# A product-key search whose last step is split between VectorE and GpSimd

## What is computed

```python
q = (xb @ w_query).reshape(t, 8, 2, 128)
s = einsum('thik,hink->thin', q, sub_keys)            # 2 x 128 scores per token and head
v_half, i_half = top_k(s, 16)                         # 16 best of each half
cand = v_half[:, :, 0, :, None] + v_half[:, :, 1, None, :]          # 16 x 16 sums
cand_idx = i_half[:, :, 0, :, None] * 128 + i_half[:, :, 1, None, :]
top_v, top_pos = top_k(cand, 16)                      # 16 best pairs
idx = take_along_axis(cand_idx, top_pos)              # <- the part that changes
g = softmax(top_v)
act = gelu(einsum('thkd,td->thk', expert_u[idx], xb))
out = einsum('thk,thkd->td', g * act, expert_v[idx])
```

## Time and profile before

| what | us |
|---|---|
| median of 3 runs | 2610.92 |
| lowest, highest | 2607.22, 2611.05 |
| the profiled execution | 2620.58 |
| its span in the trace | 2618.8 |
| TensorE busy (share of the span) | 2305.7 (88%) |
| VectorE busy | 1801.4 (69%) |
| GpSimd busy | 1169.0 (45%) |
| ScalarE busy | 638.1 (24%) |
| data moved | 705.28 MB, mean 269 GB/s |
| chain that ended last: PE, DVE, POOL, DMA, issue, ACT | 37%, 19%, 14%, 11%, 11%, 7% |

### The profile page before, as it was taken

The page is one execution under the profiler, slowest core; times in us unless marked ns, Lnnn a source line. Parts: engine busy times, 40 slices in busy tenths (PEclk is TensorE's granted clock), DMA queues, the critical chain, the costliest instruction groups (busy, mean ns, idle before and its releaser), DMA issues.

```text
span 2618.8 us, 26507 instructions
## 1 busy us (share of the span) xinstructions
PE 2305.7 (88%) x8779; PEld 1454.0 (56%) x8779; DVE 1801.4 (69%) x3184; ACT 638.1 (24%) x1564; POOL 1169.0 (45%) x978
## 2 busy tenths in 40 slices
PE   6988888998899998899989988977999999999930
PEld 1545454454467443477568877856666666644410
DVE  2657676645501888777778997578766676757698
ACT  2334435331211113311321112199111100100010
POOL 0022222221000347666532334556548878676675
PEclk8999999999999998899999999999999999999975
DMA  8211101117575669999775679989999999999998
GB/s 303 73 33 57 40 24 40 49 60 272 195 269 182 229 254 383 361 339 415 287 265 185 225 257 334 348 305 362 352 394 411 412 386 418 347 419 378 419 395 296
DMA packets 235577, 705.28 MB, mean 269 GB/s; under 512 B 22910, under 2 KB 47614, under 8 KB 234052
## 3 DMA queue, kind: packets, MB, share of 16 engines
q0 software_dynamic: 117792, 428.92, 42.6%
q1 hardware_dynamic: 116948, 272.27, 27.9%
q10 hardware_dynamic: 720, 2.62, 0.2%
HBM read 690.23 MB, written 13.50 MB: 269 GB/s over the span
## 4 chain that ended last, share of the span: by engine, by line
PE 37%; DVE 19%; POOL 14%; DMA 11%; issue 11%; ACT 7%; SPq 1%; DVEq 0%; ACTq 0%; POOLq 0%; another core or an unknown queue 0%
PE bank L959 14%; POOL arena L1786 6%; POOL arena L1778 5%; DMA arena<-in_peer_v,arena 5%; PE bank L1181 4%; PE bank L808 4%; DMA arena<-in_peer_u,arena 3%; PE bank L853 2%; ACT arena L1674 2%; DVE arena L1964 2%; PE bank L1111 2%; DVE arena L2181 2%; POOL arena L1832 2%; DVE arena L2203 2%; DVE arena L2127 1%
## 5 line engine op out<-in xcount | busy, mean ns | idle before, releaser
L1778 POOL DMA_INDIRECT arena<-in_peer_u,arena x384 | 486.3, 1266 | 624.7 <-DVE arena L2181 346.0
L2203 DVE SCALAR_TENSOR_TENSOR arena<-arena 128x1024 f32<-128x1024 f32 x381 | 498.4, 1308 | 123.2 <-DMA arena<-in_peer_v,arena 113.6
L2181 DVE CUSTOM_DVE_ANT_0 arena<-arena 128x1024 f32<-128x1024 f32 x384 | 475.9, 1247 | 149.5 <-DMA arena<-in_peer_u,arena 147.5
L1786 POOL DMA_INDIRECT arena<-in_peer_v,arena x384 | 462.0, 1203 | 242.0 <-DVE arena L2203 132.4
L959 PE MATMUL bank<-arena 128*128 128x512 f32 (+1 forms) x1472 | 510.5, 509 | 21.8 <-issue 8.1
L1181 PE MATMUL bank<-arena 128*128 128x256 f32 x2048 | 457.2, 381 | 18.5 <-ACT arena L1633 17.8
L1219 PE MATMUL bank<-arena 128*128 128x512 f32 x1024 | 455.8, 598 | 7.2 <-DMA arena<-in_peer_v 4.0
L1181 PEld LDWEIGHTS bank<-arena 128*128 128x128 f32 x2048 | 391.7, 191 | 101.0 <-issue 49.4
L959 PEld LDWEIGHTS bank<-arena 128*128 128x128 f32 x1472 | 284.1, 194 | 244.1 <-issue 206.3
L1219 PEld LDWEIGHTS bank<-arena 128*128 128x128 f32 x1024 | 196.4, 192 | 228.1 <-issue 217.1
L1633 ACT ACTIVATE arena<-bank 128x256 f32<-128x256 f32 x128 | 49.0, 384 | 597.1 <-PE bank L1181 535.1
(11 more groups left out here) (259 smaller groups left out, 2469.6 us busy)
## 6 DMA issues: line engine op xcount, KB each, us to landing
arena<-in_peer_ut SPq DMA_DIRECT2D x128, 512.0 KB
arena<-in_peer_v SPq DMA_DIRECT2D x128, 512.0 KB
arena<-in_w_in SPq DMA_DIRECT2D x22, 2048.0 KB
arena<-in_w_ada_t POOLq DMA_DIRECT2D x32, 512.0 KB, 3.8
arena<-in_w_ssd_out SPq DMA_DIRECT2D x8, 2048.0 KB
arena<-in_w_query SPq DMA_DIRECT2D x8, 2048.0 KB
arena<-in_w_ada SPq DMA_DIRECT2D x4, 2048.0 KB, 16.3
arena<-in_w_fourier SPq DMA_DIRECT2D x4, 2048.0 KB
```

The lines of the kernel that those rows point to most:

```text
L1778: nc.gpsimd.indirect_dma_start(rowbuf[slot], None, a["peer_u"], bass.IndirectOffsetOnAxis(ap=entries(IDX, k), axis=0)).then_inc(row_in[slo ...
L1786: nc.gpsimd.indirect_dma_start(rowbuf[slot], None, a["peer_v"], bass.IndirectOffsetOnAxis(ap=entries(IDX, k), axis=0)).then_inc(row_in[slo ...
L2181: V.tensor_tensor_reduce(out=rowbuf[slot], in0=rowbuf[slot], in1=h2c if item < PH else h2a[:, item // PH - 1, :], scale=1.0, scalar=0.0, o ...
L2203: STT(pv, rowbuf[slot], w, pv, ALU.mult, ALU.add).then_inc(s("vc_used"), 1)
```

## The change

The end of the search is computed in another form and in two places. The table of places now holds 16-bit values and is spread out to 1024 elements (four groups of 16 places x 16 picks), with the pick innermost. VectorE copies the split positions to 16 bits, compares them with the table, and adds one to a new semaphore `marked`. GpSimd, in `picks_for`, waits for `marked`, multiplies the result with the indices, sums over the places by halving (8, 4, 2, then the last two), combines the halves for row tiles, and counts `topk_done` or `topw_done`. For row tiles the factor 128 is put into the indices beforehand, by a small product in place of the copy of L2152. Each GpSimd step waits for the one before it (`pch`). VectorE, before it writes the indices of a search, waits for GpSimd to be done with the search before. A function `searches_before` says how many of these passes GpSimd makes before each row: all of whose searches lie on VectorE ahead of the step that frees the row's slot. The expanded table takes the place of constants of the scan (they now share one tensor, `scan_consts`) and is written by two instructions at the start of the lookup, after the scores of tile 0 are there.

```diff
+def searches_before(kind, k):
+    ...
+    passed = sum(c < context or a < apart for _, c, a in SEARCHES)
+    return max(passed, SEARCH_OF[k // TOPK] + 1)
...
-        convw = sb("convw_sb", [P, 24, TAPS])
+        scan_consts = sb("scan_consts", [P, 512])
+        convw = scan_consts[:, 192:192 + 24 * TAPS].rearrange("p (i k) -> p i k", k=TAPS)
-        places = sb("places", [P, 4, TOPK], U32)
+        places = scan_consts.bitcast(BF16).rearrange("p (g m k) -> p g m k", g=4, k=TOPK)
...
+            def picks_for(kind, k):
+                while picks_done[0] < searches_before(kind, k):
+                    m, (items, _, _) = next(picked)
+                    n, (t, h) = len(items), divmod(items[0], PH)
+                    e4 = cands[:, 0:256 * n].bitcast(BF16).rearrange("p (g m k) -> p g m k", g=2 * n, k=TOPK)
+                    number = i16fs[:, 0:2 * n * TOPK].rearrange("p (g m) -> p g m", g=2 * n)
+                    pool.wait_ge(s("marked"), m + 1)
+                    pch(TT(e4, e4, number.unsqueeze(3).broadcast_to([P, 2 * n, TOPK, TOPK]), ALU.mult))
+                    for m_left in (8, 4, 2):
+                        pch(TT(e4[:, :, 0:m_left], e4[:, :, 0:m_left], e4[:, :, m_left:2 * m_left], ALU.add))
+                    if t in WHOLE:
+                        TT(ij_all[...], e4[:, :, 0, :], e4[:, :, 1, :], ALU.add).then_inc(s("topw_done"), n)
+                    else:
+                        pch(TT(picks[...], e4[:, :, 0, :], e4[:, :, 1, :], ALU.add))
+                        pch(TT(picks[:, 0:n * TOPK], picks[:, 0:n * TOPK], picks[:, n * TOPK:2 * n * TOPK], ALU.add))
+                        nc.gpsimd.tensor_copy(entries(IDX, ...), picks[:, 0:n * TOPK]).then_inc(s("topk_done"), n)
+                    picks_done[0] = m + 1
...
             def u_row(k):
+                picks_for("u", k)
                 row_free("u", k)
...
-                CP(i16fs[:, 0:2 * n * TOPK], i16s[:, 0:2 * n * TOPK])
+                if searched["last"]:
+                    dve.wait_ge(s(searched["last"]), searched[searched["last"]])
+                if t in WHOLE:
+                    CP(i16fs[:, 0:2 * n * TOPK], i16s[:, 0:2 * n * TOPK])
+                else:
+                    TT(i16fs[...], i16s[...], radix.unsqueeze(2).broadcast_to([P, 2, n * TOPK]), ALU.mult)
...
-                ch(TT(e4, place..., flat(tijs)..., ALU.is_equal))
-                ch(TT(e4, e4, flat(i16fs)..., ALU.mult))
-                if t in WHOLE:
-                    V.tensor_reduce(ij_all[...], e4, AX.X, ALU.add).then_inc(s("topw_done"), n)
-                else:
-                    ch(V.tensor_reduce(flat(picks), e4, AX.X, ALU.add))
-                    STT(entries(IDX, ...), half[0], float(NKEY), half[1], ALU.mult, ALU.add).then_inc(s("topk_done"), n)
+                ch(CP(tij16s[:, 0:2 * n * TOPK], tijs[:, 0:2 * n * TOPK]))
+                TT(e4, places[:, 0:4:3 - n], flat(tij16s)..., ALU.is_equal).then_inc(s("marked"), 1)
...
             dve.wait_ge(s("sc_free"), 4)
+            CP(places[:, 2:4], row16)
+            ch(TS(places[:, 0:2], row16, float(TOPK), None, ALU.mult))
             top(0)
```

More of the change, by code:

```diff
@@ L223, with searches @@
 APART_TOP_AT = {42 if n == 4 else START_BETWEEN if n == 6 else 16 * n - 14: (n, n + 1) for n in range(4, 2 * PH, 2)}
+def searches():
+    at = [((0,), 0, 0), ((1,), 0, 0)] + [(pair, j + 1, 0) for j, pair in TOPS_AT.items()]
+    c, a = STEPS_DONE + 8, 0
+    for h in range(PH):
+        at.append(((3 * PH + h, 4 * PH + h), c, a))
+        c = min(CSTEPS, c + CTX_BESIDE[h])
+        if h in APART_TOP_BESIDE:
+            at.append((tuple(PH + n for n in APART_TOP_BESIDE[h]), c, a))
+        a += APART_BESIDE[h]
+    return at + [(tuple(PH + n for n in pair), CSTEPS, j + 1) for j, pair in sorted(APART_TOP_AT.items())]
+SEARCHES = searches()
+SEARCH_OF = {item: n for n, found in enumerate(SEARCHES) for item in found[0]}
+def searches_before(kind, k):
+    context, apart = 0, 0
+    before = ROW_BEFORE[ROW_NUMBER[kind, k]]
+    if before is not None:
+        kind_before, k_before = ROW_ORDER[before]
+        if k_before < PICKS:
+            context = k_before + 1 + (kind_before == "v") * LEAD
+        else:
+            apart = k_before - PICKS + 1 + (kind_before == "v") * APART_LEAD
+    passed = sum(c < context or a < apart for _, c, a in SEARCHES)
+    return max(passed, SEARCH_OF[k // TOPK] + 1)
 GATES_FIRST = (28, 36, 51)
@@ L2138, in scores_of @@
                 return src.rearrange("p (h n) -> p h n", h=2)
+            searched = {"topk_done": 0, "topw_done": 0, "last": None}
             def top(*items):
@@ L2151, in top @@
                         best16(v16[:, half, q, :], i16[:, half, q, :], src[:, half, :], sw2[:, half, :])
-                CP(i16fs[:, 0:2 * n * TOPK], i16s[:, 0:2 * n * TOPK])
+                t, h = divmod(items[0], PH)
+                if searched["last"]:
+                    dve.wait_ge(s(searched["last"]), searched[searched["last"]])
+                searched["last"] = "topw_done" if t in WHOLE else "topk_done"
+                searched[searched["last"]] += n
+                if t in WHOLE:
+                    CP(i16fs[:, 0:2 * n * TOPK], i16s[:, 0:2 * n * TOPK])
+                else:
+                    TT(i16fs[:, 0:2 * n * TOPK].rearrange("p (h k) -> p h k", h=2),
+                       i16s[:, 0:2 * n * TOPK].rearrange("p (h k) -> p h k", h=2),
+                       radix.unsqueeze(2).broadcast_to([P, 2, n * TOPK]), ALU.mult)
                 ch(TT(cand, v16[:, 0].unsqueeze(3).broadcast_to([P, n, TOPK, TOPK]),
@@ L2156, in top @@
                     best16(tv[:, q, :], tp[:, q, :], cands[:, 256 * q:256 * q + 256], cand2)
-                t, h = divmod(items[0], PH)
                 over = (d_w[:, :, TOPK * h:TOPK * h + TOPK] if t in WHOLE else
@@ L2162, in top @@
                       ALU.bitwise_and))
-                e4 = cands[:, 0:256 * n].bitcast(BF16).rearrange("p (g k m) -> p g k m", g=2 * n, m=TOPK)
-                place = places[:, 0:4:3 - n, :]
-                ch(TT(e4, place.unsqueeze(2).broadcast_to([P, 2 * n, TOPK, TOPK]),
-                      flat(tijs).unsqueeze(3).broadcast_to([P, 2 * n, TOPK, TOPK]), ALU.is_equal))
-                ch(TT(e4, e4, flat(i16fs).unsqueeze(2).broadcast_to([P, 2 * n, TOPK, TOPK]), ALU.mult))
-                if t in WHOLE:
-                    V.tensor_reduce(ij_all[:, :, TOPK * h:TOPK * h + TOPK], e4, AX.X, ALU.add).then_inc(s("topw_done"), n)
-                else:
-                    ch(V.tensor_reduce(flat(picks), e4, AX.X, ALU.add))
-                    half = picks[:, 0:n * TOPK], picks[:, n * TOPK:2 * n * TOPK]
-                    STT(entries(IDX, items[0] * TOPK, n * TOPK), half[0], float(NKEY), half[1],
-                        ALU.mult, ALU.add).then_inc(s("topk_done"), n)
+                ch(CP(tij16s[:, 0:2 * n * TOPK], tijs[:, 0:2 * n * TOPK]))
+                e4 = cands[:, 0:256 * n].bitcast(BF16).rearrange("p (g m k) -> p g m k", g=2 * n, k=TOPK)
+                TT(e4, places[:, 0:4:3 - n], flat(tij16s).unsqueeze(2).broadcast_to([P, 2 * n, TOPK, TOPK]),
+                   ALU.is_equal).then_inc(s("marked"), 1)
             def u_dot(k):
```

28 lines of the change are left out of this document (21 added, 7 removed).

## The result

The change takes **2705.65 us** (median of 4 runs, 2704.18 to 2725.17) where the kernel before takes 2610.99: a ratio of **1.0382, 95% interval 1.034 to 1.0424**. Such a ratio is made from all the runs and is not quite the quotient of the medians (here 1.0363), so a difference of two versions in microseconds comes out up to some 7 us apart by the two ways. The forecast was 2658, range 2600 to 2682: the direction was right, the size half of what came. The profiled execution took 2725.17, 19.5 above its median (that of before 9.7), so differences between the two traces overstate by some 10 us.

A forecast was written before the change was run, and what follows sets the result against it. Up to 1600 VectorE's lateness was taken to reach TensorE; the last part was bound by row and block transfers. Terms 17 + 10.7 + 20 = +47 on 2611 gave 2658 us, range 2600 to 2682.

The forecast's parts named there:

- The moved constants cost nothing: Constants moved to make room for the expanded table: no cost; only the two instructions writing the table cost, 1.3 with waits.
- VectorE's saving of 48 us: Over 21 searches VectorE is relieved of 48 us: 2.25 or 2.45 per pair, 1.4 per single item.
- GpSimd's pass undisturbed: Product and sums on GpSimd without collisions: 5.0 us for a pair of tiles 3 and 4, 6.2 for row tiles.
- Turns: Behind every search GpSimd and VectorE exclude each other; each pass step waits out one row step of about 1.2 us.
- Behind h = 0: Pairs h = 0 to 3: the fifth step's row comes 13.1 us behind the search, +4.3 each, +17.
- 850 to 997: First stage: late rows behind the pairs release ACT, and so TensorE at 997, 10.7 us later.
- the squares: Pairs up to 1600: +17 us at the squares, and TensorE's blocks end that much later.
- The pair searched at 1623 is covered by the 21.5 us of slack: VectorE's wait at 1706 for the blocks to end, 21.52 us, covers this pair's pass.
- The last part: Five pairs behind 1850: GpSimd resumes rows 9.3 us later, losing 4.0 us of transfers each, +20 us.
- the passes hide: Rival, chance 0.18: passes with turns take under about 3.8 us, rows resume no later than before, 2577 us.
- do not collide: Rival, chance 0.10: passes cost 6.2 and 5.0 us but no turns occur, 2609 us.
- GpSimd is the bound in the last part: Rival, chance 0.10: GpSimd's queue never catches up, five passes count in full, 46 in place of 20, 2684 us.

The follow-up runs named there:

- all on VectorE: The change with product and tree run on VectorE behind the comparison, not on GpSimd: 1.013; with the arena on byte 24320, 1.0042.
- all passes late: The change with GpSimd's passes mostly behind 4 to 10 further rows: 1.0137 (arena on 24096), 1.0149 (24128), 1.007 (24320).
- the arena back: The change with 224 unused bytes ahead of the arena, putting it on byte 24320 as in the kernel before: 2681.40 us, 1.0234.

## Why the prediction was half right

**"The moved constants cost nothing" is the step that failed.** The merged tiles moved the arena off its multiple of 256, and where the DMA engines are all busy they move 403 GB/s in place of 418. The window of before behind 1850:

```profile
1850.00:2619.00 769.00, 656.27 (x2024) 385.04 (x2022) 550.79 (x806) 67.24 (x139) 536.73 (x440) 0.93 0.97 387
```

Estimated from it: 387 GB/s over 769 us are 298 MB; at 403 in place of 418 that takes 26 us more. By the ratios it is 37 us for the kernel before moved by 32 bytes and 25 moved by 128, 23 for all on VectorE (1.013 against 1.0042), 39 for the change (1.0382 against 1.0234), but only 17 to 21 with all passes late (1.0137 and 1.0149 against 1.007). No term, rival or bound held this. With the arena back the change is at 1.0234, 61 us above before, and 2611 x 1.0234 = 2672 lies inside the range.

**The rest, +47 forecast, +61 measured**, by the terms:

- *VectorE's saving of 48 us*: right in size and eaten. The `u_dot`s grew from 475.9 to 496.9 us in all, the `v_add`s from 498.4 to 521.2. VectorE's busy time is 1806.9 beside 1801.4.
- *GpSimd's pass undisturbed*: 1.85 was taken for the product; 1.92 measured, and 1.7 by what it holds VectorE up; 2.4 for three halvings with their gaps, 2.41 measured. By the Trainium skill (GPSIMD Engine Reference, Elementwise — side-by-side cycle accounting: 4497 ns for 2048 elements in 32 bits) the product would be 2.25, an estimate; the 1.85 from GpSimd's own rows was nearer.
- *Turns*: right, instruction by instruction (the fence behind the pair (2,3)). It is what the Trainium skill (SBUF — State Buffer, Who interferes with whom) calls a lock held for the whole instruction; the trace agrees: 1.7 us of waiting beside the product.
- *Behind h = 0*, where the forecast put the fifth step 13.1 us behind the search:

```profile
1390.56 2.88 POOL L1820 TENSOR_TENSOR arena<-arena 128x1024 bf16<-128x1024 bf16 x1 [22.89 <-DVE arena L2237]
1393.53 4.13 POOL L1822 TENSOR_TENSOR arena<-arena 128x512 bf16<-128x512 bf16 x3
1397.80 1.10 POOL L1824 TENSOR_TENSOR arena<-arena 128x64 f32<-128x64 bf16 x1
1399.05 0.98 POOL L1848 DMA_INDIRECT arena<-in_peer_v,arena  x1
...
1390.40 6.22 DVE L2267 SCALAR_TENSOR_TENSOR arena<-arena 128x1024 f32<-128x1024 f32 x3
...
1403.44 1.28 DVE L2267 SCALAR_TENSOR_TENSOR arena<-arena 128x1024 f32<-128x1024 f32 x1 [4.71 <-DMA arena<-in_peer_v,arena]
```

  13.04, with a wait of 4.71 where 4 to 6 stood. The searches h = 1 and 2 come 4.0 and 4.3 us later each (4.3 was forecast), the pair behind h = 2 only 2.2. From h = 0 to h = 7 the change loses 11.8 us, 13.1 with the arena back; forecast 17.
- *850 to 997*: forecast 10.7. TensorE is released at 1017.41, 19.7 later, and at 1006.74, 9.1 later, with the arena back; taken from the first search of each trace 18.1 and 10.9. The first row behind the pair (2,3) is used 14.1 us behind it (14.8 was forecast), but a second wait for a row, 5.29 us at 916.86, was not foreseen: with four slots the round of rows starts late and goes on late. How much of the spread between traces is this and how much chance stays open.
- *997 to h = 0*: no search lies there, and the forecast has nothing. In the five traces with the arena on a multiple of 256 and passes on GpSimd, 6.6 to 14.6 us are lost there (11.5 by the change with the arena back), in the twelve others -4.9 to 3.0. No run explains it. So that 27.7 was forecast at the squares and 30 came is in part luck: the terms before h = 0 spread by 15 us over the traces with the same passes (5.6, 18.7 and 20.6), and only those behind it come out alike.
- *"The pair searched at 1623 is covered by the 21.5 us of slack"*: VectorE's slack is still there, but the time is lost by another way, and between the searches at 1637 and 1854 both traces lose 6 to 8 us. First before, then the change, where TensorE (L1196, L1230) starts the gate units:

```profile
1702.07 1.02 PE L1196 MATMUL bank<-arena 98*128 98x512 bf16 x4 [0.35 <-ACT arena L1633]
```

```profile
1740.81 1.89 PE L1230 MATMUL bank<-arena 98*128 98x512 bf16 x4 [8.11 <-DMA arena<-features_far]
...
1746.88 0.42 DVE L2448 TENSOR_TENSOR arena<-arena,bank 128x256 f32<-128x256 f32 x1 [21.33 <-ACT arena L1697]
```

  The blocks end 31.0 us later than before and the gate units start 38.7 later: TensorE now waits for the features' way back from HBM, which is asked for some 12 us ahead of the blocks' end in both kernels. In the four traces with this pair's pass right behind its search, the last row goes out 6 to 9 us ahead of the blocks' end and the wait is 4.9 to 8.1 us; in the fourteen others it goes out 16 to 20 us ahead and the wait is 0.3 to 2.0. So the late rows seem to hold this transfer up; no run tests it alone.
- *The last part*: 4.0 a search forecast; with the arena back 5.1, 6.0, 10.3 and 7.4 from one search to the next. In the DMA windows 20 us of reduced share stand behind a search, as forecast (17). The sum is 30 where 20 stood: the mechanism was right and its price too low. Windows around one such search, arena back, and then the two of before behind the same search:

```profile
2140.00:2150.00 10.00, 10.00 (x32) 5.89 (x31) 9.28 (x41) 0.74 (x2) 4.60 (x6) 1.00 1.03 420
2150.00:2160.00 10.00, 10.00 (x39) 7.22 (x38) 9.83 (x16) 0.38 (x1) 6.66 (x4) 1.00 0.80 292
2160.00:2170.00 10.00, 10.00 (x34) 6.18 (x33) 5.71 (x7) 0.77 (x2) 8.64 (x8) 1.00 0.58 180
2170.00:2180.00 10.00, 10.00 (x38) 6.93 (x37) 5.92 (x8) 0.38 (x1) 8.73 (x8) 1.00 1.01 385
```

```profile
2100.00:2110.00 10.00, 10.00 (x37) 6.77 (x36) 9.82 (x14) 0.38 (x1) 5.35 (x4) 1.00 0.78 268
2110.00:2120.00 10.00, 10.00 (x37) 6.54 (x36) 8.34 (x12) 0.77 (x2) 8.74 (x8) 1.00 1.00 377
```

  Against 420 GB/s the windows with the arena back fall short by 128, 240 and 35, over 10 us each: 9.6 us lost. Those of before fall short by 152 and 43 and lose 4.6. The search at 2306 meets something else besides. Once in each of eight traces looked at, the requests for blocks pause for 17.2 us, in before from 2263.1, where rows are in flight. With the arena back the pause begins at 2305.2, right at this search, and the DMA engines stand still; by the same count 16.7 us are lost around it, where before loses 7.9:

```profile
2311.00:2316.00 5.00, 5.00 (x17) 2.90 (x16) 5.00 (x5) 0.38 (x1) 4.77 (x4) 1.00 0.00 0
```
- *Rivals*: "the passes hide" and "do not collide" fell by the trace. "GpSimd is the bound in the last part" is nearer to the time measured (2684), for a wrong reason: moving passes back in the queue, with the same work on GpSimd, took some 60 us away. What is left for it is at most 3.4 us for a late pass.

## What to carry to other kernels

Where a tile ahead of the DMA buffers changes its size, look at where the buffers start afterwards: a multiple of 256 bytes in each partition was worth 0.7 to 1.5% here. Put the relief of a busy engine where the helper is idle: with the same passes the kernel was 61 us above before when they stood ahead of the row gathers that they held up, and 18 when they stood behind four to ten of them (1.0234 and 1.007). And if a long step starves a queue of transfers, two halves with work between them can be worth more than a faster step.
